# Eight sample streams of a hybrid decoder's sparse attention: one block with a schedule written out, instead of a loop of blocks

## The reference, cut to what matters

```
kc, vc = compress(concat(past pages, new rows))     # 255 compressed keys and values
    # per 16 rows: two 64x64 products ("first" and "second" half), summed with the neighbour's,
    # + bias, silu, times w2; the keys RMS-normed with k_norm
s = q kc * scale ; p = softmax(s) ; o_cmp = p vc
ps = p summed over the 4 heads of a group, added up to 65 blocks of 64 positions
idx = top 16 blocks (block 0 and the last two forced)
o_sel = softmax(q k_sel | blocks in idx) v_sel      # all 4096 positions are scored, blocks masked
o_win = softmax(q k_win | last 512 positions) v_win
o = g0 * o_cmp + g1 * o_sel + g2 * o_win            # then times silu(az), into the output projection
```

## Time and profile before

| | us |
|---|---|
| median of 3 runs (2436.68 to 2440.33) | 2437.31 |
| the profiled execution | 2436.53 |
| its span, first to last instruction | 2434.8 |
| PE busy | 2143.9 (88%) |
| DVE, ACT, POOL busy | 851.7, 697.7, 154.1 |
| DMA | 316.19 MB, mean 130 GB/s |

### The profile page before, as it was taken

The page is one execution under the profiler, slowest core; times in us unless marked ns, Lnnn a source line. Parts: engine busy times, 40 slices in busy tenths (PEclk is TensorE's granted clock), DMA queues, the critical chain, the costliest instruction groups (busy, mean ns, idle before and its releaser), DMA issues. The chain is left out here.

```text
span 2434.8 us, 34702 instructions
## 1 busy us (share of the span) xinstructions
PE 2143.9 (88%) x12851; PEld 1740.2 (71%) x12851; DVE 851.7 (35%) x1644; ACT 697.7 (29%) x1337; POOL 154.1 (6%) x192
## 2 busy tenths in 40 slices
PE   7999999999988887799857889888986569999998
PEld 7999999999985555655533554455444369999998
DVE  6233255233323334456502233223323432233232
ACT  6332223333323222156511222122212031133221
POOL 0000000000001000000011121012111001010000
PEclk9999999999998887599978889988997779999999
DMA  5542333333313333111136657665753272222330
GB/s 188 172 152 75 93 98 112 98 107 98 113 65 125 129 132 121 47 53 57 61 125 233 218 191 241 226 226 186 240 198 114 63 283 94 70 90 76 98 103 25
DMA packets 167331, 316.19 MB, mean 130 GB/s; under 512 B 22365, under 2 KB 71902, under 8 KB 164130
## 3 DMA queue, kind: packets, MB, share of 16 engines
q1 hardware_dynamic: 156536, 297.33, 36.9%
q10 hardware_dynamic: 10666, 17.05, 2.1%
HBM read 281.53 MB, written 41.05 MB: 132 GB/s over the span
## 5 line engine op out<-in xcount | busy, mean ns | idle before, releaser
L250 PE MATMUL mm<-x_hi,w_hi 128*128 128x288 f32 x1696 | 369.1, 299 | 14.3 <-DVE w_lo L381 14.3
L250 PE MATMUL mm<-x_lo,w_hi 128*128 128x288 f32 x1696 | 364.1, 296 | 0.0
L250 PE MATMUL mm<-x_hi,w_lo 128*128 128x288 f32 x1696 | 364.1, 296 | 0.0
L250 PEld LDWEIGHTS mm<-x_hi,w_hi 128*128 128x128 f32 x1696 | 274.8, 190 | 15.9 <-issue 12.2
L250 PEld LDWEIGHTS mm<-x_lo,w_hi 128*128 128x128 f32 x1696 | 274.5, 190 | 0.0
L250 PEld LDWEIGHTS mm<-x_hi,w_lo 128*128 128x128 f32 x1696 | 274.2, 189 | 0.0
L381 DVE TENSOR_TENSOR w_lo<-w_raw,w_hi 128x1024 fp32r<-128x1024 f32 x106 | 129.8, 1225 | 386.4 <-ACT w_hi L280 386.4
L1529 PE MATMUL s_pH<-wide,cw_sample 128*128 128x512 f32 x512 | 239.4, 624 | 9.7 <-PEq L86 9.7
L1970 PE MATMUL o_mm<-o_feat_hi,o_w_hi 128*128 128x288 f32 x1024 | 225.7, 302 | 24.5 <-DVE o_feat_lo L2045 17.7
L1970 PE MATMUL o_mm<-o_feat_lo,o_w_hi 128*128 128x288 f32 x1024 | 222.0, 299 | 0.0
L1970 PE MATMUL o_mm<-o_feat_hi,o_w_lo 128*128 128x288 f32 x1024 | 221.6, 299 | 0.0
(11 more groups left out here) (395 smaller groups left out, 2487.6 us busy)
## 6 DMA issues: line engine op xcount, KB each, us to landing
wide<-pages SPq DMA_DIRECT2D x256, 256.0 KB, 4.1
w_raw<-w_in SPq DMA_DIRECT2D x106, 512.0 KB, 4.0
s_kv<-pages SPq DMA_DIRECT2D x192, 256.0 KB, 4.9
s_kv<-pages ACTq DMA_DIRECT2D x64, 256.0 KB, 7.3
o_w_raw<-w_out SPq DMA_DIRECT2D x16, 1024.0 KB, 7.8
o_w_raw<-ple_gate SPq DMA_DIRECT2D x16, 1024.0 KB, 6.7
m_state<-state SPq DMA_DIRECT2D x4, 2056.0 KB, 11.9
state_sample<-m_state SPq DMA_DIRECT2D x4, 2056.0 KB, 6.7
```

The lines of the kernel that those rows point to most:

```text
L250: last = nc.tensor.matmul(mm[:, s % 3, y, 0:HALF], w[:, m % RING, kk, :], f[:, k, y * HALF:(y + 1) * HALF], start=k == 0 and i == 0, stop= ...
```

## The change

`sample_turn` and `combine_samples` go. `attend_samples` is one block with all eight turns written out in Python, so that each engine has one list, and no barrier stands between samples.

- **PE's list** is an order written by hand: window scores first, the second layer and the turned keys of the sample's own compression now stand in its own turn (before, they stood in the turn ahead), and `hidden` of the next sample is cut into steps of 1, 2, 3 or 8 matmuls placed between the parts.
- **Value products** (compressed, window, selection): for each 128 positions two matmuls, one for each half of the array's columns: 64 rows of probabilities with the 128 value columns of their two groups, instead of one of 128 rows with 256 columns.
- **Mask and maximum**: one `tensor_tensor_reduce` per chunk instead of `tensor_tensor` and `tensor_reduce`; likewise for the new rows of the window.
- **Second layer**: `cw2` is put on the diagonal of a 128x128 matrix, 8 matmuls instead of 16.
- **Branches**: per branch DVE scales the 128x128 result by a column of gate over sum, masked by `diag`, in one instruction; PE gathers the three branches with `pick` into a 128x64 tile (`gather`), and DVE multiplies it into `az`. No store to DRAM, no `o_scratch`. The columns of gates are made once at the start by 3 matmuls.
- **Compression on DVE**: sum with bias in one instruction (`hidden_sum`), product (`hidden_gated`), square and one reduction for the norm; `k_norm` comes as the scale of ACT's copy. POOL keeps three instructions at the start.
- **Loads**: `load_pages` has no loop and fixed places in the table. Key and value pages of sample b+1 are issued in turn b: quarters 0 and 2 by SP, 1 by ACT at the end of the turn, 3 by ACT after the window's exponentials of turn b+1. Compression pages of sample b+2: 16 pages behind `hidden(1)`, 8 behind `hidden(3)`, 8 more behind quarter 0.

The diff, cut to the core:

```diff
+            def compressed_values(b):
+                pe.wait_ge(ct_ready, b + 1)
+                if b:
+                    pe.wait_ge(out_ready, b)
+                for nt in range(2):
+                    n = min(P, NC - nt * P)
+                    for gp in range(2):
+                        last = mm(pO[half(gp), 0, 0:P], pcT[0:n, nt, half(gp)], vc[0:n, nt, gp * P:(gp + 1) * P], start=nt == 0, stop=nt == 1)
...
+            def values(b, q):
+                pe.wait_ge(t_copied, PARTS * b + q + 1)
+                if q == 0:
+                    pe.wait_ge(x_ready, 3 * b + 1)
+                for i in range(4 if q < NQ else 1):
+                    for gp in range(2):
                         if q < NQ:
-                            last = mm(S.pO[:, 0, 0:256], S.probT[:, q % 2, i, :], S.kvp[:, 4 * q + i, 256:512], start=q == 0 and i == 0, stop=False)
+                            v0 = 256 + gp * P
+                            last = mm(pO[half(gp), 0, 0:P], probT[:, q % 2, i, half(gp)], kvp[:, 4 * q + i, v0:v0 + P],
+                                      start=q == 0 and i == 0, stop=False)
...
+            for b in range(NB):
+                c = b + 1
+                window_scores(b)
+                hidden(c, 0, range(8))
+                if b:
+                    gather(b - 1)
+                second_layer(b)
+                hidden(c, 1, range(8))
+                keys_turned(b)
+                hidden(c, 2, range(0, 2))
+                compressed_scores(b)
+                hidden(c, 2, range(2, 5))
+                compressed_turned(b)
+                hidden(c, 2, range(5, 7))
+                compressed_values(b)
+                window_turned(b)
+                hidden(c, 2, range(7, 8))
+                hidden(c, 3, range(0, 2))
+                window_values(b)
+                block_bias(b)
+                for j in range(PARTS):
+                    scores(b, j)
+                    if j in (2, 4, 6):
+                        hidden(c, 3, range(1 + j // 2, 2 + j // 2))
+                hidden(c, 3, range(5, 8))
+                for j in range(PARTS + 1):
+                    if j < PARTS:
+                        turned(b, j)
+                    if j >= 1:
+                        values(b, j - 1)
+            gather(NB - 1)
...
         @block.sync
...
+            sp.wait_ge(h_done, 2)
+            load_comp(sp, 1, 0, HP)
+            load_kv(sp, 0, 2)
+            sp.wait_ge(h_done, 4)
+            load_comp(sp, 1, HP, NPG)
+            for b in range(NB):
+                if b + 2 < NB:
+                    sp.wait_ge(h_done, 4 * (b + 1) + 2)
+                    load_comp(sp, b + 2, 0, HP)
+                if b + 1 < NB:
+                    sp.wait_ge(wo_done, b + 1)
+                    sp.dma_start(wnd[:], a["win_pages"][b + 1]).then_inc(wnd_in, 16)
+                if b + 2 < NB:
+                    sp.wait_ge(h_done, 4 * (b + 1) + 4)
+                    load_comp(sp, b + 2, HP, HP + QP)
+                if b + 1 < NB:
+                    sp.wait_ge(pv_done, PARTS * b + 2)
+                    load_kv(sp, b + 1, 0)
+                if b + 2 < NB:
+                    load_comp(sp, b + 2, HP + QP, NPG)
+                if b + 1 < NB:
+                    sp.wait_ge(pv_done, PARTS * b + 6)
+                    load_kv(sp, b + 1, 2)
...
         @block.scalar
...
+            for b in range(NB):
+                c = b + 1
+                act.wait_ge(wm_ready, b + 1)
+                s_.activation(pw[:, 0:WIN], pS[:, 1, :], ACT.Exp, bias=mx[:, 13:14], accum_out=rs[:, 13:14])
...
+                if b:
+                    act.wait_ge(pv_done, PARTS * b)
+                    load_kv(act, b, 3)
+                split(c, 0)
+                act.wait_ge(kv_done, b + 1)
...
+                split(c, 2)
+                act.wait_ge(mx_ready, b + 1)
+                for j in range(PARTS):
+                    if j == 2:
+                        split(c, 3)
+                    if j in (4, 5, 6):
+                        sigmoid(c, j - 4)
+                    s_.activation(chunk(j), chunk(j), ACT.Exp, bias=mx[:, 11:12], accum_out=rs[:, j:j + 1]).then_inc(p_ready, 1)
+                if c < NB:
+                    act.wait_ge(pv_done, PARTS * b + 4)
+                    load_kv(act, c, 1)
...
         @block.vector
...
+                    if j < NQ:
+                        blocked = lambda r: r.rearrange("p (k x) -> p k x", x=BLK)
+                        by = bias[:, 8 * j:8 * j + 8].unsqueeze(2).to_broadcast([P, 8, BLK])
+                        last = v.tensor_tensor_reduce(blocked(chunk(j)), blocked(pS[:, j % 2, :]), by, 1.0, -3e38, ALU.add, ALU.max, mx[:, j:j + 1])
...
+                for j in range(PARTS):
+                    dve.wait_ge(t_done, PARTS * b + j + 1)
...
+                        last = v.tensor_copy(probT[:, j % 2], pT[:, j % 2, :].rearrange("p (n r) -> p n r", r=P))
...
+                    if j == 2:
+                        hidden_sum(c)
+                    if j == 6:
+                        hidden_gated(c)
...
+def load_pages(eng, ptab, pages, dst, part, first, begin, end, sem):
+
+    numbers = [eng.value_load(ptab[0:1, first + i:first + i + 1], min_val=0, max_val=pages.shape[0] - 1) for i in range(begin, end)]
+    for i, page in zip(range(begin, end), numbers):
+        eng.dma_start(dst[:, i, :], pages[bass.ds(page, 1), :, part * CH:(part + 1) * CH].rearrange("x p c -> p (x c)")).then_inc(sem, 16)
```

More of the change, by code:

```diff
@@ L1452, in load_pages @@
-def load_pages(sp, ptab, pages, dst, part, first, begin, end, sem):
-    AHEAD = 8
-    assert begin % AHEAD == 0 and end % AHEAD == 0
-    with sp.Fori(begin // AHEAD, end // AHEAD) as i:
-        numbers = [sp.value_load(ptab[0:1, bass.ds(first + i * AHEAD + j, 1)], min_val=0, max_val=pages.shape[0] - 1)
-                   for j in range(AHEAD)]
-        for j, page in enumerate(numbers):
-            sp.dma_start(dst[:, bass.ds(i * AHEAD + j, 1), :].rearrange("p x c -> p (x c)"),
-                         pages[bass.ds(page, 1), :, part * CH:(part + 1) * CH].rearrange("x p c -> p (x c)")).then_inc(sem, 16)
@@ new lines, in values, with gather @@
+                last.then_inc(pv_done, 1)
+            def gather(b):
+                pe.wait_ge(x_ready, 3 * b + 3)
+                for y in range(3):
+                    last = mm(pO[:, 0, 256:320], out[:, y, :], pick[:], start=y == 0, stop=y == 2)
+                last.then_inc(xa_done, 1)
+            pe.wait_ge(gate_parts, 1)
+            pe.wait_ge(mine_ready, 1)
+            for y in range(3):
+                last = mm(pO[:, 0, y * NB:(y + 1) * NB], spreadg[:, y, :], mine[:], start=True, stop=True)
@@ new lines, in _ @@
+            last.then_inc(gates_done, 1)
+            pe.wait_ge(cw1_in, 16)
+            pe.wait_ge(B.comp0_in, 16 * NPG)
+            for i in range(4):
+                hidden(0, i, range(8))
+            pe.wait_ge(consts, 1)
+            for b in range(NB):
[28 more added lines that the diff above has]
+                        values(b, j - 1)
@@ L1641, in _, with split @@
             step = Chain(act, act_step)
[L1643 to L1644 removed]
+            def split(c, i):
+                if c >= NB:
                     return
[L1646 to L1649 removed]
@@ new lines, in split, with sigmoid @@
+                act.wait_ge(h_done, 4 * c + i + 1)
+                s_.activation(first[half(x), cc * CH:(cc + 1) * CH], pH[0:64, x, :], ACT.Copy)
+                s_.activation(second[half(x), cc * CH:(cc + 1) * CH], pH[64:128, x, :], ACT.Copy).then_inc(h_split, 1)
+            def sigmoid(c, part):
+                if c >= NB:
+                    return
+                if part == 0:
+                    act.wait_ge(hid_sum, c + 1)
+                    step(s_.activation(gate, first[:, 0:NH], ACT.Exp, scale=-1.0))
+                elif part == 1:
+                    step(s_.activation(gate, gate, ACT.Ln, bias=1.0))
+                else:
+                    s_.activation(gate, gate, ACT.Exp, scale=-1.0).then_inc(sig_ready, 1)
```

652 lines of the change are left out of this document (278 added, 374 removed).

## The result

The changed kernel takes **2294.3 us** (median of four runs, 2292.25 to 2295.08) against 2437.86 for the kernel before on the same chip: a ratio of 0.9409, 95% interval [0.9392, 0.9425]. The forecast was 2258, with a range of 2212 to 2312. The profiled execution took 2292.25 us, with a span of 2290.5.

A forecast was written before the change was run, and what follows sets the result against it. It had PE busy 70.6 of 82 us per turn. First layer to 1257.0, turn 0 to 1334, six turns of 63.5 to 1715, last turn to 1771.5, then 3.4: 1774.9 instead of 1954.0, 179.1 less, so 2258 us; range 2212 to 2312.

The forecast's parts named there:

- the start's two waits: In turn 0, PE waits twice for sample 1's compression pages, 6 and 8 us; the second group lands at 1290.5.
- The main case: Whole kernel: full turns of 63.5 us, likeliest time 2258 us, between 2235 and 2285, chance 0.45.
- The wait for keys: In a full turn after hidden(1), PE waits 2.8 us until the keys come at 21.0 us.
- The step that failed: Last 8 compression pages of a full turn: issued until 10.4 us, landed by 20.6, wanted by PE at 21.6.
- a rival at 0.18: Pages come late in each turn: two queues at once cost 5 us, turns of 68.5 us, 2293 us; chance 0.18.
- ACT's chain: Rival: ACT's loads ahead of the keys are 2.6 us shorter each, turns of 58.5 us, 2223 us; chance 0.2.
- Value products: Paired products in the value phase: a chunk costs 0.87 + 0.58 for turns = 1.45 us instead of 2.17.
- The rival in which they don't hide at all: Weight loads of short value-product pairs cost 0.8 us per chunk, 6 us per turn, 2306 us; chance 0.12.
- Mask and maximum in one: Fused DVE instruction per chunk of scores takes 0.75 us, between 0.68 and 1.37; without gain, + 11 us.
- The page loads are hidden in a turn: In the kernel before, page loads are hidden in a turn, but they hold their queue; ACT stands for 9.6 us.
- The last turn: Last turn without cover matmuls: 56.5 us, with 20 until keys, 9 for compressed chain and choice of blocks.
- SP as the bound: Rival: SP's queue of 48 pages per turn at 2.1 us each, turns of 101 us, 2507 us; chance 0.03.

The follow-up runs named there:

- square of four: Kernel before with value products paired, eight value pages per turn moved from SP to ACT, both, or neither: 2421.12, 2435.75, 2383.0 and 2437.9 us.
- e1_order: Changed kernel with the second half of the compression pages loaded in one go ahead of the eight value pages on SP: 2245.71 us, 0.9208 of before.
- e3_unpaired: Changed kernel with value products unpaired, one matmul of 256 columns instead of two of 128: 2295.65 us, 0.9432 of before.
- e2_quarter: Changed kernel where each key-and-value page of samples 1 to 7 brings 32 of its 128 rows: 2263.19 us, 0.9273 of before.
- f1_reads_first: Changed kernel, page load order kept, but SP reads the next three groups' 24 page numbers before waiting for their places: 2249.66 us, 0.9228 of before.
- f4_best: Changed kernel with compression pages first, sample 1's shared by SP and ACT, sigmoid one chunk later, ACT's last loads moved back: 2229.35 us, 0.9144 of before.

## Why the prediction was right, and where it was off

The direction, the parts and the range held: turns without a gap between them, products in pairs, the fused instruction, the start's two waits. The main case, 2235 to 2285, did not, and it was wrong by its own sign ("if PE waits for pages in the later turns"): PE does so in each of six. The range held because its upper end was taken from a rival. The median came 36.3 us above the forecast. In the profiled execution the next block starts at 1811.9 and not at 1774.9, 37.0 later: 2.9 in the start (the first layer begins at 1229.7, not 1227.5, and ends at 1259.9), 6.2 in turn 0, 6 x 4.94 = 29.7 in the full turns, less 1.8 at the end. (What follows takes 2.2 less than before, and the median lies 2.1 above that execution and not 0.8.) In turn 0 the pages of the second wait were there at 1297.4, forecast 1290.5.

**The full turn, step by step.** Window scores to the end of hidden(1): forecast 18.2, measured 17.4, since the second layer takes 2.0 and not 2.4. The wait for keys: forecast 2.8, measured none. From the keys' turns to the first score: forecast 13.3, measured 21.7, of which 5.7 are the wait for pages and 1.9 the slow clock. Scores with their cover: 10.0, measured 11.1. The value phase: 17.9, measured 18.3. Together 68.5 for 63.5 (62.2 by these steps, and 1.3 for handovers and half a cold start at the turn's beginning, where `hidden(0)` took 7.13 us, at a granted clock of 1.00; the rows that the 1.7 for a whole one came from, 8.68 against 7.13, give 1.55).

**The step that failed** is the one that let the pages come just in time: "issued until 10.4 of the next turn, and the longest landing was 10.2 us: 20.6, and PE wants them at 21.6". Measured: issued until 11.5, landed 12.2 later, at 23.7, and PE wanted them at 18.0. So the wait of 5.7 is 1.1 from the issue, 2.0 from the landing, 3.6 from PE being early, less the margin of 1.0 that I had counted. The largest is the third, and it was my other error that hid it: I had PE wait 2.8 us for the keys just before, and thought of that as a cost of its own, when it was also the cover of the pages. The case stood as a rival at 0.18 with 68.5 us per turn and 2293 in all, and it is what happened. That its numbers are met so closely is luck: its 5 us were set and not derived, and the turn came to 68.5 by 7.6 of wait and slow clock, less 3.6 that PE was early, and smaller misses. Against it I had put the 391 GB/s of the earlier trace rows. That was the wrong witness: the changed kernel reaches 388, and the six turns average 249. The question was not how many bytes a turn moves but when the last eight pages are asked for, which SP's list in order of time would have told.

**ACT's chain** was on time, the rival at 0.2. The reads of page numbers (first line: eight of them, 0.275 us each, started from 1473.5 to 1477.2) began under ACT's last exponentials:

```profile
L1890 ACTq TENSOR_LOAD <-ptab x8: 273/275/288, 1473.5 to 1477.2; - x8
...
1476.00 0.19 ACT L1742 ACTIVATION_READ_ACCUMULATOR s_scores<-s_scores,s_mx 128x1 f32 x1
1477.89 5.31 ACTq L1892 DMA_DIRECT2D s_kv<-pages  x8
1483.25 0.69 ACT L1704 ACTIVATE s_scores<-s_pS,s_mx 128x512 f32<-128x512 f32 x1 [7.06 <-DVE s_mx L1810]
```

The last exponential's read ends at 1476.2 and eight numbers are read by 1477.9; I had 9.0 us for reads and issues together behind the last exponential, and the first load was done 2.8 us into the turn, not 5.6. The price of a page was right, its place on the engine was not. The keys came before 1497.84, 17.4 us into the turn; forecast were 21.0.

**Value products.** A period of 1.61 to 1.64 us, not 1.45: turns 0.59 from start to start (forecast 0.58), sixteen passes in 1.02 (forecast 0.87). So two halves run together at 0.128 us a pair of passes where the prompt's rows gave 0.11, and 8 x 0.17 = 1.4 us a turn were missing. Whether the missing 0.17 a chunk is a part of the weight loads was not settled. The rival in which they don't hide at all (0.8 us a chunk more) is out: unpaired, a chunk takes 2.16 us, paired 1.61. Its sum was wrong too: 6.4 less 3.3 of waits plus 1.3 are 4.4 us a turn and not 6, so 2293 and not 2306, and the range's upper end of 2312 was built on it. Sixteen weight loads and sixteen passes took 1.02 us, with the loads busy for 0.85 of it (1544.33 and after). In the value phase the wait for the fifth exponential was forecast at 1.8 and is 1.27; the 3.3 us of waiting forecast there are 1.9 in the trace (1.27 and two of 0.3), which hid the longer period.

**Mask and maximum in one**: 0.69 + 0.08 = 0.77 against 0.75. Its worth, forecast 11 us, is 9.7 without the page wait and 5.4 with it.

**The bound of the kernel before.** "The page loads are hidden in a turn" was true and yet misleading: the square of four shows that SP's list ended with PE's. The forecast for the whole change was not hurt, since the streams removed both ends, but whoever had tried the pairs alone, on that sentence, would have forecast 43 us or more and got 16.

**The last turn**, 54.0 to its last product against 56.5, and 4.1 to the next block against 3.4. Two errors cancel in it: the keys came 14.4 us into it and not 20, and the compressed chain with the choice of blocks took 13.4 and not 9. No run shows the 1.2 GHz at which the sum put a part of the last turn's value products: in the changed kernel they ran from 1794.0 to 1806.4, at a granted clock of 1.00 (1793 to 1808), and it was the stretch before them, 1768.2 to 1793, that had 0.67. **SP as the bound** (0.03) did not come: a page costs 1.1 us as forecast.

## What to carry to other kernels

Before pricing an edit, lay the lists of all engines and queues that end in the same barrier or wait beside each other and note the slack of each: an edit is worth no more than the slack of the second, as the pairs were worth about 0 us in the changed kernel, 16 in the kernel before, 37 with the pages in the better order and 53 in the kernel before with a shorter list for SP. In these runs pages were late mostly by the time at which SP's queue asked for them: the changed kernel waited 33.1 us for pages over six turns, the same bytes in the better order 0, a quarter of the value pages' bytes in the old order 9.6. Mean rates and totals had not shown it, so order a queue's issues by when their data are wanted. And a wait that you forecast on the critical path is cover for other things: when you drop it from the sum, check again what was hidden behind it.

## What the runs showed of the hardware

- A wait of 5.7 us of PE cost 1.9 us more behind it: two matmuls of 512 columns (four passes) took 3.78 us at a granted clock of 0.51, against 1.88 in e1_order. Behind waits of 0.3 to 1.3 us they took 1.98 or 1.99 (e3_unpaired, e2_quarter, f1_reads_first, f4_best). Behind 2 us it went either way (1.98 behind 2.05 in e3_unpaired, 2.90 and 2.79 behind 2.03 and 2.13 in e2_quarter), and behind 2.72 and 3.13 they took 3.68 and 3.63 (the same two runs).
- Eight pages of 256 KB took up to 12.5 us from issue to landing with four groups of eight around them, and the engines moved 388 GB/s for 20 us (1484 to 1504); the earlier trace rows had shown such a rate for 4 us.
- ACT's queue read its next eight page numbers from 1473.5 on (the last read started at 1477.2), while its earlier exponentials ran until 1476.2.
- Two 128-column products on the two halves of the array took 0.128 us a pair (1.02/8), including two weight loads, where one of 256 columns took 0.216 (1.73/8).
- One DVE pass over 1020 elements that adds two tensors and a bias in their own order took 1.27 us, and one that multiplies two and writes the product in another order 1.96 (L1757 and L1763 of the changed kernel, the mean of four each). That the order is the reason was not tested by itself.
